# A hybrid attention and mixture-of-experts layer on one core: expert weights asked for in halves, slot lists from tables in memory, and four edges reordered

## The reference

```python
q_nope, q_rope, latent, k_rope, f_q, f_k, f_v, log_f, m_q, gates = project_in(h, pos, ...)
o_mla, o_fox, o_mem = attend_block(...)        # latent, forget-gate and memory attention
y = (gates[:, :, 0] * (o_mla @ w_br_mla) + gates[:, :, 1] * (o_fox @ w_br_fox)
     + gates[:, :, 2] * (o_mem @ w_br_mem)) @ w_out
x1 = layer_norm(ALPHA * h + y, ln1_g, ln1_b)
# moe_ffn: 64 experts of width 256, sigmoid scores, 4 of 8 groups kept, the best 8 experts per token
w = w / jnp.sum(w, axis=-1, keepdims=True) * 2.5
acc + g_col[:, None] * ((silu(t @ wg) * (t @ wu)) @ wd)        # for each expert
out = layer_norm(ALPHA * x1 + routed + shared, ln2_g, ln2_b)
```

## Time and profile before

| | us |
|---|---|
| median of three runs | 1192.73 (1192.25 to 1194.02) |
| profiled execution | 1193.32 |
| its span | 1191.5 |
| TensorE busy | 1145.8 (96%) |
| VectorE busy | 514.9 (43%) |
| ScalarE busy | 205.3 (17%) |
| POOL busy | 53.4 (4%) |
| granted TensorE clock, mean | 0.99 |
| HBM read and written | 302.2 MB and 10.7 MB |

### The profile page before, as it was taken

How to read it: one execution, slowest core, us unless ns; L and a number is a source line. 1 busy time by engine, 2 the same in 40 slices (tenths; PEclk the granted TensorE clock), 3 DMA queues, 4 the chain that set the end, 5 groups by cost and what they waited for, 6 DMA issues and landing times.

```text
span 1191.5 us, 17467 instructions
## 1 busy us (share of the span) xinstructions
PE 1145.8 (96%) x6434; PEld 662.2 (56%) x6434; DVE 514.9 (43%) x1415; ACT 205.3 (17%) x383; POOL 53.4 (4%) x59
## 2 busy tenths in 40 slices
PE   6999999999999979999999999999999999999994
PEld 3445546666666645547655555555555555555551
DVE  1242004445555513337554454455445345445426
ACT  0222115554333300001000110110110010011011
POOL 2100000000000000001100000000000000000000
PEclk9999999999999989999999999999999999999998
DMA  8442055223554456846199999999999999999971
GB/s 297 130 144 71 1 179 186 86 96 126 196 167 164 163 185 204 334 191 203 43 360 374 377 380 395 373 369 391 376 374 399 374 377 386 392 374 376 388 315 55
DMA packets 84724, 308.97 MB, mean 259 GB/s; under 512 B 14664, under 2 KB 26480, under 8 KB 58552
## 3 DMA queue, kind: packets, MB, share of 16 engines
q1 hardware_dynamic: 67840, 274.98, 59.0%
q0 software_dynamic: 5696, 15.47, 4.5%
q10 hardware_dynamic: 11136, 17.83, 4.3%
HBM read 302.20 MB, written 10.74 MB: 263 GB/s over the span
## 4 chain that ended last, share of the span: by engine, by line
PE 92%; DVE 3%; DMA 1%; ACT 1%; issue 1%; ACTq 0%; DVEq 0%
PE ps_P L1230 19%; PE ps_P L938 10%; PE ps_V L1255 10%; PE ps_V L1244 10%; PE ps_P L847 6%; PE ps_V L1166 5%; PE ps_S L1244 5%; PE ps_T L840 4%; PE ps_P L855 4%; PE ps_V L1175 3%; PE ps_T L1219 3%; PE ps_S L947 2%; PE ps_P L979 1%; PE ps_V L1207 1%; PE ps_S L1237 1%; PE ps_V L906 1%
## 5 line engine op out<-in xcount | busy, mean ns | idle before, releaser
L1230 PE MATMUL ps_P<-arena,branch_out 128*64 128x256 f32 (+1 forms) x2176 | 233.6, 379 | 0.6 <-DVE branch_out L1861 0.6
L1230 PEld LDWEIGHTS ps_P<-arena,branch_out 128*64 128x64 f32 (+1 forms) x2176 | 151.2, 135 | 90.9 <-issue 19.2
L938 PE MATMUL ps_P<-xT,weight_ring 128*128 128x384 f32 x384 | 135.3, 487 | 0.0
L1867 DVE TENSOR_TENSOR branch_out<-branch_out,ps_P 128x256 f32<-128x256 f32 x33 | 13.9, 421 | 266.3 <-PE ps_P L1230 266.3
L1244 PE MATMUL ps_V<-weight_ring,branch_out 128*128 128x512 f32 x264 | 124.1, 592 | 0.0
L1255 PE MATMUL ps_V<-arena,branch_out 128*64 128x512 f32 (+1 forms) x544 | 120.6, 598 | 0.0
L1422 ACT ACTIVATE weight_ring<-ps_V,merge 128x512 f32<-128x512 f32 x66 | 45.3, 687 | 427.6 <-PE ps_V L1255 427.6
L1888 DVE TENSOR_TENSOR x_sb<-x_sb,ps_V 128x512 f32<-128x512 f32 x136 | 93.5, 687 | 22.9 <-PE ps_V L1244 17.4
L938 PEld LDWEIGHTS ps_P<-xT,weight_ring 128*128 128x128 f32 x384 | 68.9, 191 | 34.1 <-issue 0.4
L1244 PEld LDWEIGHTS ps_V<-weight_ring,branch_out 128*128 128x128 f32 x264 | 47.9, 191 | 47.3 <-issue 47.3
L1166 PE MATMUL ps_V<-branch_out,weight_ring 128*128 128x384 f32 x192 | 65.4, 504 | 7.6 <-DVE merge L1806 7.2
(11 more groups left out here) (304 smaller groups left out, 1180.3 us busy)
## 6 DMA issues: line engine op xcount, KB each, us to landing
arena<-w_e_gate SPq DMA_DIRECT2D x68, 1024.0 KB, 8.5
arena<-w_e_up SPq DMA_DIRECT2D x68, 1024.0 KB, 10.5
arena<-w_e_down SPq DMA_DIRECT2D x68, 1024.0 KB, 7.2
weight_ring<-w_in SPq DMA_DIRECT2D x12, 1024.0 KB, 8.6
weight_ring<-w_in ACTq DMA_DIRECT2D x8, 1024.0 KB, 6.1
gates<-arena ACTq DMA_DIRECT2D x24, 192.0 KB, 3.0
xT<-gates ACTq DMA_DIRECT2D x24, 192.0 KB, 7.3
arena<-cache_fox_k SPq DMA_DIRECT2D x8, 512.0 KB, 3.6
```

Source lines behind the costliest of these rows:

```text
L938: last = mm(out[:, 0:T], slot[:, k % 4, m * P:(m + 1) * P], xT[:, k, :], start=(k == 0), stop=(k == KD - 1))
L1230: last = mm(bank[r:r + wide, 0:256], xgT[q][:, k, r:r + wide], w[h][:, k, :], start=(k == 0), stop=(k == KD - 1))
```

## The change

- **Halves.** The gate and up matrices of an expert are loaded as two transfers of half the contraction (k 0 to 3, 4 to 7), 4 KB for each partition instead of 8. TensorE signals the middle of each product too (`gate_half`, `up_half`), and SP asks for a first half then.
- **Tables.** Lists 0 to 6 are made as before (`LISTED` = 7). From list 7 on, VectorE works out for each token's eight experts a row number, slot x 59 + step (`place_rows`, after step 0), and the pair token, weight (`fill_rows`, after step 1). POOL writes them with 24 indirect DMAs of 128 rows of 8 bytes into six cleared tables in device memory, and reads these back (`raw`). VectorE adds the six (`merge_rows`, in step 4), and from then on only copies a column to `idx` (`copy_row`). `slot_tokens`, `build_onehot` and `copy_slots` vanish from steps 4 to 29, with the columns for the pieces. The tables are cleared by six DMAs on SP's queue early in the kernel.
- **Edge 1.** The transposes of input tiles 1 and 2 both come before `lat` 1.
- **Edge 2.** Each `mq` product comes between `qn` and its two `qa`.
- **Edge 3.** Gates 0 to 3 of the merge get four buffers of their own (in `fkc` and `mkc`), loaded by ScalarE after the exponential of the last score unit; gates 4 to 23 use the eight in `xT`.
- **Edge 4.** The last layer norm: the closing additions sum their rows, ScalarE squares and takes the root, and VectorE applies the norm from a separate buffer; the three tiles are added first, then applied.

The core of the diff:

```diff
@@ load_pair @@
+                for sems, w, dst, half_done, all_done in ((gate_loaded, w_eg, ew_gate, gate_half, gate_done), (up_loaded2, w_eu, ew_up, up_half, up_done)):
+                    for part, finished in ((slice(0, 4), half_done), (slice(4, KD), all_done)):
+                        if later:
+                            sp.wait_ge(finished, n - 1)
+                        for h, e in enumerate(experts):
+                            sp.dma_start(dst[2 * q + h][:, part], w[bass.ds(e, 1)].rearrange("e (p k) f -> p (e k) f", p=P)[:, part]).then_inc(sems[q], 16)
@@ plan @@
-    for j in range(TT):
-        s += [("T", "x", j, 0), ("T", "x", j, 1), ("P", "lat", j)]
+    s += [("T", "x", 0, 0), ("T", "x", 0, 1), ("P", "lat", 0)]
+    s += [("T", "x", j, half) for j in (1, 2) for half in range(2)]
+    s += [("P", "lat", 1), ("P", "lat", 2)]
...
     for h in range(0, H, 2):
-        s.append(("P", "qn", h // 2))
-        if h:
-            s += [("P", "qa", h - 2), ("P", "qa", h - 1)]
-    s += [("P", "qa", H - 2), ("P", "qa", H - 1)]
-    s += [("P", "mq", m) for m in range(4)]
+        s += [("P", "qn", h // 2), ("P", "mq", h // 2), ("P", "qa", h), ("P", "qa", h + 1)]
@@ scalar, score unit @@
+                    if n == len(U) - 1:
+                        act.wait_ge(done["T"], done_at("T", "cfk", NB - 1, 1))
+                        act.wait_ge(done["T"], done_at("T", "cmk", NB - 1, 1))
+                        for i in range(4):
+                            load_gate(i)
@@ gpsimd @@
+            gather(3, 1)
+            gather(4, 0)
+            pool.wait_ge(rows_cleared, 16 * TABLES)
+            pool.wait_ge(rows_ready, 2)
+            for k in range(TOPK):
+                for j in range(TT):
+                    n, to = j * TOPK + k, j + k % 2 * TT
+                    if k >= 2:
+                        pool.wait_ge(rows_stored[to], 16 * (k // 2))
+                    pool.indirect_dma_start(rows_dram[to], bass.IndirectOffsetOnAxis(ap=row_idx[:, n:n + 1], axis=0), entries[:, n, :], None, ...)
+                if k == TOPK // 2 - 1:
+                    gather(5, 1)
+            for to in range(TABLES):
+                pool.wait_ge(rows_stored[to], 16 * TOPK // 2)
+                pool.dma_start(raw[:, to, :], rows_dram[to]...[:, 2 * LISTED:2 * STEPS]).then_inc(rows_loaded, 16)
+            gather(6, 0)
+            gather(7, 1)
+            gather(8, 0)
@@ vector, new functions @@
+            def place_rows():
+                link(V.tensor_tensor(dest, mask, cc("keys").unsqueeze(1).to_broadcast([P, TT, E]), ALU.mult))
...
+                for j in range(TT):
+                    ins = V.max(key8[:, j, :], dest[:, j, :])
+            def fill_rows():
+                for j in range(TT):
+                    link(V.tensor_tensor(chosen, dest[:, j, :].unsqueeze(1).to_broadcast([P, TOPK, E]),
+                                         key8[:, j, :].unsqueeze(2).to_broadcast([P, TOPK, E]), ALU.is_equal))
+                    link(V.tensor_tensor(chosen, chosen, weight[:, j, :].unsqueeze(1).to_broadcast([P, TOPK, E]), ALU.mult))
+                    link(V.tensor_reduce(weight8[:, j, :], chosen, AX, ALU.add))
+            def merge_rows():
+                dve.wait_ge(rows_loaded, 16 * TABLES)
...
+            def copy_row(n, par):
+                V.tensor_copy(idx[:, par:par + 1], info[:, bass.ds(n, 1), 0:1].rearrange("p o c -> p (o c)")).then_inc(idx_ready, 1)
@@ vector, end @@
+                    V.tensor_tensor_reduce(xv, xv, tiles[k % 3][:, :], 1.0, 0.0, ALU.add, ALU.add, row_sum[:, k:k + 1]).then_inc(last_added, 1)
+            for j in range(TT):
+                link(ln2_scale(V, j))
+                link(inverse(j))
+                ln2_shift(V, j).then_inc(out_ready[j], 1)
@@ scalar, end @@
+                fn(squares, x_sb[:, j, :], ACT.Square, bias=neg_mean[:, j:j + 1], accum_out=square_sum[:, j:j + 1]).then_inc(square_ready, 1)
+                fn(rst[:, j:j + 1], square_sum[:, j:j + 1], ACT.Sqrt, bias=eps, scale=1.0 / D).then_inc(rstd1_ready, 1)
```

More of the change, by code:

```diff
@@ L52 @@
 EARLY = PAIRS // 2 - 2
-COLS = E + MORE + 16
+LISTED = 7
+COLS = 2 * LISTED
+TABLES = 2 * TT
+STEPS = LAST + 4
 ALPHA = 2.0 ** 0.25
@@ L450, in build @@
         wsum = N.take(TT)
-        counts, chunks, first, more_n = (N.take(1) for _ in range(4))
+        counts, chunks, first = (N.take(1) for _ in range(3))
         over = N.take(10)
-        offs = N.take(MORE)
-        since, is_in, begun, shift = (N.take(MORE) for _ in range(4))
-        pcol = [N.take(TT, 12) for _ in range(2)]
+        since, is_in, begun = (N.take(MORE) for _ in range(3))
+        pcol = [N.take(TT, 6) for _ in range(2)]
+        weight, dest, far, place = (N.take(TT, E) for _ in range(4))
+        chunks_of = N.take(E)
+        token1 = N.take(TT)
+        far_base = N.take(E)
+        raw = R_W[:, 6912:6912 + TABLES * 2 * (STEPS - LISTED)].rearrange("p (j x) -> p j x", j=TABLES)
+        none = R_W[:, 7680:7680 + STEPS - LISTED].unsqueeze(2)
+        key8, weight8 = N.take(TT, TOPK), N.take(TT, TOPK)
+        chosen = R_W[:, 6400:6912].rearrange("p (k e) -> p k e", k=TOPK)
+        entries = N.take(TT * TOPK, 2)
         info = N.take(LAST + 4, 2)
@@ L482, in build @@
         gates_dram = nc.dram_tensor("gates", (GATES, P, T), F32, kind="Internal").ap()
+        rows_dram = [nc.dram_tensor(f"slot_rows{j}", (P * STEPS, 2), F32, kind="Internal").ap() for j in range(TABLES)]
         x1_dram = nc.dram_tensor("x1_rows", (T, D), F32, kind="Internal").ap()
@@ L568, in build @@
         last_added = sem("last_added")
[L569 to L570 removed]
+        out_ready = [sem(f"out_ready{j}") for j in range(TT)]
+        mean_ready = sem("mean_ready")
+        square_ready = sem("square_ready")
         d_of = {
@@ L1382, in _ @@
                         act.wait_ge(done["P"], done_at("P", "g", GATES - 1))
-                        for i in range(KD):
+                        for i in range(4, 4 + KD):
                             load_gate(i)
-                    if n + KD < GATES:
+                    if n >= 4 and n + KD < GATES:
                         act.wait_ge(free["V"], done_at(*st))
@@ L1894, in _ @@
             build_onehot(3, 1)
-            with dve.Fori(0, EARLY) as i:
+            pair(0, 0)
+            place_rows()
+            pair(1, 1)
+            fill_rows()
+            for n in range(2, 6):
+                pair(n, n % 2)
+            with dve.Fori(3, EARLY) as i:
                 for q in range(2):
```

232 lines of the change are left out of this document (127 added, 105 removed).

## The result

| | median | runs |
|---|---|---|
| kernel before | 1192.7 us | 1192.3 to 1194.0 |
| changed kernel | 1182.6 us | 1180.8 to 1184.5 |

The ratio is 0.9913, with a 95% interval from 0.9896 to 0.9931: 0.9% faster, 10 us. The forecast was 33.6 us. The profiled execution of the changed kernel took 1182.85 us, 10.5 less than that of the kernel before.

A forecast was written before the change was run, and what follows sets the result against it. TensorE, busy in 96% of the span, was taken to bound the kernel. Terms 14.9 + 10.4 + 3.5 + 1.3 + 0.5 + 3.0 = 33.6 us gave 1159.1 us; range 1156 to 1168, 8 times in 10.

The forecast's parts named there:

- the new tables: Expert steps 0 to 5: VectorE's table blocks hidden, POOL's scatters landing in time; cost 0, upper end a 9 us stall.
- I take 0: Scatters in the expert steps: 0 us for the wait on late tables and 0 for their load on the weight stream.
- The record's own signs of a wrong forecast: TensorE waiting for weights, step 4 or 5 longer than 17.6 us, or the clock dropping in the merge.
- Slot lists: Expert steps 4 to 29 lose TensorE's slot-list product, 26 x 0.575: 14.9 us gained.
- The weight stream: Expert steps: 394 GB/s asked at 16.97 us a step, some 20 us of lead; cost 0, last step up to 1.6.
- VectorE's blocks hidden: Steps 0 and 1: place_rows, about 4.8 us, and fill_rows, 7.1 us, fit VectorE's 8.15 us gap; merge_rows in step 4, 2 us.
- The merge: Merge of the branches at L1166: TensorE's 7.2 us wait and 3.2 us of half clock go, 10.4 us gained.
- Early edges: Queries and inputs, early in the kernel: less TensorE waiting on copies, 3.5 us and 1.3 us gained.
- Router: Before the first slot list: slot columns shrink from 64 to 14, shortening VectorE's chain, 0.5 us gained.
- Tail: Last layer norm, from the first closing addition to the last store: VectorE's statistics go, 3.0 us gained.
- Halves: Expert gate and up weights asked for about 1.8 us sooner; costed at 0, as nothing waits for them.
- rival 1: Step 4 or 5: scatters land slowly, tables come late, VectorE then TensorE stops; some 9 us, 1168 us, chance 11%.

The follow-up runs named there:

- 1: Changed kernel without its 24 scatters, so steps from 7 on gather no tokens: 1161.3 us.
- 2: Changed kernel with the 24 scatters replaced by 24 gathers over the same indices, from the tables into the chip's entries: 1183.1 us.
- 13: Changed kernel with the 24 scatters replaced by 24 GpSimd fills of an unused tile, no transfer: 1161.5 us.
- 10: Changed kernel with all 24 scatters in one train, each of 16 partitions instead of 128: 1185.0 us.
- 4: Changed kernel with three scatters behind each of gathers 4 to 11 and 13 slot lists made the old way: 1164.4 us.
- 7: Changed kernel with six scatters behind each of gathers 4 to 7 and 9 slot lists made the old way: 1167.9 us.
- 9: Six scatters behind each gather, 9 old-way lists, later groups waiting for the up product's end, against the changed kernel: 1162.0 us, on another chip 1162.8.
- 5: Changed kernel with the 24-scatter train behind gather 8, 13 old-way lists, TensorE's first ten steps written out: ratio 1.0007 to the kernel before.
- 6: Changed kernel with the 24-scatter train behind gather 8, 13 old-way lists, TensorE's first ten steps looped: ratio 1.0007 to the kernel before.
- 8: Changed kernel with the expert steps' gate and up weights loaded whole instead of in halves: 1183.7 us.
- the edges alone: Kernel before with only the input, query and early merge-gate load edges; slot lists, loads and tail as before: 1179.9 us.
- 14: Changed kernel with six scatters a step beside the down product, 9 old-way lists, and gate and up weights loaded whole: 1161.5 us.

## Why the prediction was wrong

The step that failed is the one on **the new tables**. It priced the 24 scatters in three ways: GpSimd's time (one each 0.99 us or more, 27 us, to 660), the landing and the wait of VectorE behind it, and the bytes that they put into the DMA queues. It didn't price them for TensorE, and TensorE was where they cost: 22.3 us. Nothing in the trace of before shows indirect transfers in a row; each gather there stands alone in its step. The sentence "I take 0" held only for the costs named. The experiments put the cost on indirect transfers by GpSimd that follow one another (1, 2, 13), counted by instruction and not by rows or direction (2, 10), and by how many stand together beside a gate and up product: three cost nothing, six 1.9 us (4, 7, 9), and not on code, place or halves (5, 6, 8). The record's own signs of a wrong forecast missed it as well: they named waits for weights, steps 4 and 5 and the clock in the merge, and it was step 3.

**That the phase matters is shown (7 and 9); why is argued.** TensorE's matmuls are free of it at first, and how long may depend on how fast it works through its instructions. Windows from the first scatter to where TensorE falters (the counts in brackets are matmuls and weight loads), in the changed kernel and in experiment 5:

```profile
618.17:632.35 14.18, 13.50 (x72) 7.08 (x69) 8.10 (x22) 0.69 (x1) 11.04 (x11) 1.00 0.86 324
```

```profile
682.63:689.30 6.67, 6.67 (x62) 4.17 (x57) 0.00 (x0) 0.69 (x1) 5.14 (x6) 1.00 1.01 379
```

The times differ by a factor of two, 14.2 and 6.7 us, the counts little: 141 and 119. Behind that point the changed kernel starts 42 in 20 us (632 to 652). This is what one would see if TensorE had a stock of some 100 instructions in hand and the train let only two or three more through in a microsecond: 100 + 2.9 x 6.7 = 119, 100 + 2.9 x 14.2 = 141. Two constants fitted to two windows prove nothing by that. A gate and up product takes 128 in 6.91 us; the rest of a step about 90 in 10.5. By that, three scatters (3.8 us) beside the gate product use 70, six (7.7 us) about 135, six beside the down product 66, with 111 and 122 to be had in 3.8 and 7.7 us: no cost, a small cost, no cost, as in experiments 4, 7 and 9. The Trainium skill (Runtime: NRT & Kernel Launch, "Instruction fetch mechanics") says that each engine reads its instructions ahead in blocks of 16 KiB by a DMA queue of its own, mostly hidden. The rows of q8 agree in the block size (0.08 MB in 5), but the looped kernel, with next to no such fetches, has the same hole, so the reading of code isn't what starves. Against the stock of instructions speaks that the signals are late first: ScalarE's first scaling of step 2's down product comes at 630.94 where the pattern of the step before asks for 627.41, and in experiment 5 its activation of the gate product at 690.04 where the step before asks for 686.13. Both were due while TensorE's matmuls still followed one another without a gap, to about 631.7 and 689.3. So it may be TensorE's signals that are held back, and its matmuls only behind them. What GpSimd's indirect transfers and TensorE share, no run here tells; nor was it tried whether the recording of the trace has a part in it.

The other points, by the steps of the record:

- **Slot lists, 14.9 us: right.** Steps 4 to 31 take 16.97 us.
- **The weight stream: right.** 394 GB/s were asked for; the window from 700 to 1100 has 395 GB/s, a share of 1.01, and TensorE busy for 400.00 of 400 us. Gate weights land after 9.6 us for 8.5. The Trainium skill's limit near 358 GB/s for one core (DMA: Bandwidth & Descriptors, "Where 436 GB/s comes from") is passed by these 395 too. Only the last step waits for its up weights, 0.3 us of the 0 to 1.6 allowed.
- **VectorE's blocks hidden: right.** `fill_rows` is done at 617.3; moved by the 14.8 us of the earlier start, the record's 632.4 is 617.6. `merge_rows` takes 2 us and doesn't wait.
- **The merge, 10.4 us: right.** Its `out` product starts 14.4 us earlier, 4.0 of which it inherits; no wait and no lower clock in it.
- **Early edges, 4.8 us: measured 4.0** in the changed kernel's trace, 2.7 in that of the edges alone; between the traces of the changed kernel's variants the start of step 0 differs by 2.4 us (575.0 to 577.4), so a difference of this size can't be told.
- **Router, 0.5: right** (14.8 less the 14.4 of the output product). **Tail, 3.0: right.** From the start of step 32 to the end 37.1 us for 40.1.
- **Halves, 0: right** (experiments 8 and 14).

So 14.8 + 14.9 + 3.0 - 22.3 = 10.4 us, which is the difference of the two profiled spans (1191.5 and 1181.1). Of the rivals none happened; rival 1 had the right instructions and the wrong victim. What was missing from the record's list was a rival in which the scatters hold up an engine that doesn't wait for them.

## What to carry to other kernels

Price a new row of GpSimd's indirect transfers for the engines that don't wait for it as well: leave gaps, three at a time here, or put them beside a stretch in which TensorE has few, long instructions. Groups of six gave 14.7 us over the changed kernel, and a single wait on TensorE's progress 6 more. When an engine stands for "issue" and nothing else is busy but one engine, look at what that one engine is doing. And where a change adds a pattern that the trace doesn't contain even once, an honest bound for it isn't that of the single operation.

## What the runs showed of the hardware

- 24 indirect transfers by GpSimd, one every 1.28 us, slow TensorE from 7 (experiment 5) to 14 us (changed kernel) after their start, to 42 matmuls and weight loads in 20 us (632 to 652, changed kernel), and its signals reach the others late (26 us in experiment 5). The same in both directions and for 16 or 128 rows; not for fills of a like length (12 in 12.14 us).
- An indirect transfer of 16 rows keeps GpSimd for 0.84 to 0.89 us, one of 128 mostly for 0.97 to 1.02: nearly all of it is fixed.
- Plain stores of 128 pieces of 8 bytes landed after 11.5 us beside a full weight stream, where a gather of the kernel before landed after 4.4. The Trainium skill (DMA: Bandwidth & Descriptors, "Specifications") says that transfers under 512 B become read-modify-writes; the long landing fits, but isn't proof of it. The size of the pieces alone doesn't give it: the scatters of experiment 4 write pieces of 8 bytes too, landed after 6.0 us (median), and left the weight stream its rate.
